# Expert weights fetched as couples of parts, in rows of 16 KB instead of 8 KB

## What is computed

```python
def expert_block(args):
    xb, e = args
    hb = jax.nn.silu(xb @ w_g[e]) * (xb @ w_u[e])
    return hb @ w_d[e]
...
y = y_pad[dest] * gates[order][:, None].astype(y_pad.dtype)
out = jnp.zeros((t, d), xt.dtype).at[token_idx[order]].add(y)
```

## Time and profile before

| | |
|---|---|
| median of 3 runs | 1832.19 us (1831.79 to 1833.74) |
| the profiled execution | 1832.44 us |
| its span, first to last instruction | 1830.6 us |
| around the span | 1.8 us |
| TensorE busy over the span | 98% |
| VectorE, ScalarE busy | 71%, 57% |
| DMA, mean over the span | 246 GB/s |
| granted clock of TensorE, mean | 0.994 |

### The profile page before, as it was taken

How to read it: one execution, slowest core, us unless ns; L and a number is a source line. 1 busy time by engine, 2 the same in 40 slices (tenths; PEclk the granted TensorE clock), 3 DMA queues, 4 the chain that set the end, 5 groups by cost and what they waited for, 6 DMA issues and landing times.

```text
span 1830.6 us, 22547 instructions
## 1 busy us (share of the span) xinstructions
PE 1789.4 (98%) x9273; PEld 1514.8 (83%) x9273; DVE 1292.6 (71%) x1295; ACT 1034.5 (57%) x1069; POOL 103.3 (6%) x106
## 2 busy tenths in 40 slices
PE   8998999999999999999999999999999999999998
PEld 7987788888788887888899888888888899888886
DVE  5876799999999998655468755546554778755554
ACT  5554698889888886544344444435443544444442
POOL 1010110111010100000000000000000100000000
PEclk9999999999999999999999999999999999999999
DMA  9842689999999999555464355545554754446550
GB/s 350 257 150 104 257 348 417 410 400 417 397 414 411 415 408 370 198 184 184 147 252 149 137 186 184 187 169 217 187 187 168 267 194 151 173 161 220 185 188 39
DMA packets 69885, 450.25 MB, mean 246 GB/s; under 512 B 11276, under 2 KB 11640, under 8 KB 18577
## 3 DMA queue, kind: packets, MB, share of 16 engines
q1 hardware_dynamic: 59744, 425.44, 61.5%
q0 software_dynamic: 9824, 22.78, 4.0%
q10 hardware_dynamic: 208, 0.54, 0.1%
HBM read 448.50 MB, written 14.16 MB: 253 GB/s over the span
## 4 chain that ended last, share of the span: by engine, by line
PE 78%; DMA 8%; DVE 7%; ACT 3%; issue 2%; POOL 0%; ACTq 0%; POOLq 0%; SPq 0%; DVEq 0%
PE PS L484 22%; PE PS L486 22%; PE PS L485 21%; DMA ring<-in_wt 8%; PE PS L1607 6%; DVE wl L462 4%; PE PS L1613 2%; PE PS L2223 1%; ACT wh L453 1%; DVE morel L462 1%; PE PS L523 1%; PE PS L2749 1%; ACT yr L1955 1%; PE PS L1598 1%; ACT moreh L453 1%
## 5 line engine op out<-in xcount | busy, mean ns | idle before, releaser
L462 DVE TENSOR_TENSOR wl<-ring,wh 128x2048 fp32r<-128x2048 f32 (+1 forms) x348 | 791.0, 2279 | 293.5 <-ACT wh L453 293.1
L453 ACT ACTIVATE wh<-ring 128x2048 fp32r<-128x2048 f32 (+1 forms) x348 | 661.6, 1907 | 307.2 <-PE PS L486 270.1
L484 PE MATMUL PS<-wh,XTh 128*128 128x512 f32 x952 | 379.2, 398 | 6.0 <-DVE XTl L567 3.0
L486 PE MATMUL PS<-wh,XTl 128*128 128x512 f32 x952 | 372.5, 391 | 0.0
L485 PE MATMUL PS<-wl,XTh 128*128 128x512 f32 x952 | 372.1, 391 | 0.0
L484 PEld LDWEIGHTS PS<-wh,XTh 128*128 128x128 f32 x952 | 179.4, 188 | 43.8 <-DVE wl L462 4.0
L486 PEld LDWEIGHTS PS<-wh,XTl 128*128 128x128 f32 x952 | 179.2, 188 | 38.1
L485 PEld LDWEIGHTS PS<-wl,XTh 128*128 128x128 f32 x952 | 179.6, 189 | 35.3 <-issue 0.2
L1607 PE MATMUL PS<-wh,xgT 128*128 128x512 f32 x384 | 155.4, 405 | 0.6 <-DVE xgT L1816 0.4
L1607 PE MATMUL PS<-wl,xgT 128*128 128x512 f32 x384 | 151.1, 394 | 0.0
L484 PE MATMUL PS<-XTh,wh 128*128 128x256 f32 (+2 forms) x480 | 138.0, 288 | 0.1
(11 more groups left out here) (445 smaller groups left out, 2546.4 us busy)
## 6 DMA issues: line engine op xcount, KB each, us to landing
ring<-in_wt SPq DMA_DIRECT2D x392, 1024.0 KB, 5.9
park<-in_wt SPq DMA_DIRECT2D x6, 1024.0 KB, 5.8
xtmp<-in_norm_g POOLq DMA_DIRECT2D x6, 512.0 KB, 5.7
ring<-in_wt SPq DMA_DIRECT2D x4, 512.0 KB, 7.6
toep<-frow POOLq DMA_DIRECT2D x1, 2048.0 KB, 55.6
y_d<-in_zero POOLq DMA_DIRECT2D x1, 2048.0 KB, 37.2
yy<-y_d POOLq DMA_DIRECT2D x4, 512.0 KB, 5.3
bv<-in_b_b_in POOLq DMA_DIRECT2D x1, 1536.0 KB, 7.6
```

Of the source, the lines that this page charges most:

```text
L453: s.activation(k.pieces(i)[0], k.raw(i), ACT.Copy).then_inc(*k.w_hi.up(i))
L462: v.tensor_tensor(l, k.raw(i), h.bitcast(F32), ALU.subtract).then_inc(*k.w_lo.up(i))
L484: pe.matmul(o, lhsT=left[0], rhs=right[0], start=first, stop=False)
L486: return pe.matmul(o, lhsT=left[1], rhs=right[0], start=False, stop=final)
```

## The change

Expert parts that aren't parked are fetched two at a time, as a couple: one DMA of 2 MiB brings two parts that follow each other. For this, `packed_weights` lays the rows of a couple side by side, so that each partition reads 16 KB in one row. There are three places for couples, `two0`, `two1` and `two2`: four of the five ring places make two of them, and the room of XT makes the third (with the old parks park2 and park3 gone from there; park2 moves to the fifth ring place). A couple is issued when the second part of the couple three before it has been split. Both its parts count as landed together. Outside the experts the ring works as before. The first five parts of f0 wait for other parts than before, and ScalarE waits, ahead of its first write to XT in f0, until the last expert part has been split.

```diff
 def packed_weights(inputs):
 
-    out = []
-    for nk, w, blocks in weight_parts()[0]:
...
+    parts, at = weight_parts()
+    firsts, out = set(couples(at)), []
...
+        out.append(x.reshape(nk, 128, w).transpose(1, 0, 2).reshape(128, -1))
+    rows = [np.concatenate(out[i:i + 2], 1) if i in firsts else x for i, x in enumerate(out) if i - 1 not in firsts]
+    return np.concatenate([x.reshape(-1) for x in rows])
+
+
+def couples(at):
+
+    m = at["moe"]
+    return [m + 5, m + 8, m + 10] + list(range(m + 14, at["f0"], 2))
...
+        self.two = [at(f"two{x}", o, 2 * PART) for x, o in enumerate((9768, 15912, 5672))]
...
+        if self.moe_part(i):
+            n, x = self.couple(i)
+            return self.two[n % 3][:, PART * x:PART * x + PART]
...
+    def left_place(self, i):
+
+        f0 = self.at["f0"]
+        if self.moe_part(i):
+            n, _ = self.couple(i)
+            return self.couples[n - 3] + 1 if n > 2 else (self.at["moe"] - 1, None, self.at["moe"] + 2)[n]
+        if f0 <= i < f0 + RING:
+            return (self.at["moe"] + 7, f0 - 6, f0 - 5, f0 - 4, f0 - 3)[i - f0]
+        return i - RING
...
+    elif k.moe_part(i):
+        n, x = k.couple(i)
+        if x == 0:
+            if n == 1:
+                sp.wait_ge(*k.moe.pe.at("lg"))
+            else:
+                sp.wait_ge(*k.w_lo.at(k.left_place(i)))
+            sp.dma_start(k.two[n % 3], k.couple_in(i)).then_inc(*k.d[f"two{n % 3}"].up(i))
+        return
     elif i >= RING:
-        sp.wait_ge(*k.w_lo.at(k.line[k.line.index(i) - RING]))
+        sp.wait_ge(*k.w_lo.at(k.left_place(i)))
...
     split_hi(s, k, k.after[a])
+    s.wait_ge(*k.w_lo.at(k.at["f0"] - 1))
     enter_high(s, k, m, 0, 0)
```

More of the change, by code:

```diff
@@ L181, in packed_weights @@
 def packed_weights(inputs):
-    out = []
-    for nk, w, blocks in weight_parts()[0]:
-        x = np.concatenate([inputs[name][at][r0:r0 + 128 * nk, c0:c1] for name, at, r0, c0, c1 in blocks], 1)
-        out.append(x.reshape(nk, 128, w).transpose(1, 0, 2).reshape(-1))
-    return np.concatenate(out)
+    parts, at = weight_parts()
+    firsts, out = set(couples(at)), []
+    for nk, w, blocks in parts:
+        x = np.concatenate([inputs[name][at_][r0:r0 + 128 * nk, c0:c1] for name, at_, r0, c0, c1 in blocks], 1)
+        out.append(x.reshape(nk, 128, w).transpose(1, 0, 2).reshape(128, -1))
[4 more added lines that the diff above has]
+    return [m + 5, m + 8, m + 10] + list(range(m + 14, at["f0"], 2))
 def split_plan(n, spans):
@@ L212 @@
 LANDINGS = ("ident", "cst", "rows", "x0", "x1", "rel", "ones", "mem", "b", "toep", "sel", "gmix", "gmem", "ga", "gl", "gc", "late", "gf", "gn", "wr", "xn", "zero", "yy", "bt", "ki",
-            "wsp", "bsp", "bcol", "bv", "gain", "out", "w0", "half0", "half1", "park0", "park1", "park2", "park3", "park4", "park5", "w1", "w2", "w3", "w4", "xg0", "xg1", "yd0", "yd1",
+            "wsp", "bsp", "bcol", "bv", "gain", "out", "w0", "half0", "half1", "park0", "park1", "park2", "park4", "park5", "two0", "two1", "two2", "w1", "w2", "w3", "w4", "xg0", "xg1", "yd0", "yd1",
             "rest_xg", "rest_w", "rest_yd")
@@ L237, in __init__ @@
         first = self.at["moe"]
-        self.parked = {first + SPLIT: "park0", first + SPLIT + 1: "park1", first + 7: "park2", first + 8: "park3",
-                       first + 12: "park4", first + 13: "park5"}
-        self.line = [i for i in range(len(self.parts)) if i not in self.parked]
+        self.parked = {first + SPLIT: "park0", first + SPLIT + 1: "park1", first + 7: "park2", first + 12: "park4",
+                       first + 13: "park5"}
+        self.couples = couples(self.at)
         self.part_at = [0] + list(itertools.accumulate(128 * nk * w for nk, w, _ in self.parts))
@@ L345, in __init__ @@
         self.parks = {"park0": here("park0", 14768, PART), "park1": here("park1", 12720, PART),
-                      "park2": at("park2", 15912, PART), "park3": at("park3", 17960, PART),
+                      "park2": at("park2", 13864, PART),
                       "park4": here("park4", 6824, PART), "park5": here("park5", 0, PART)}
+        self.two = [at(f"two{x}", o, 2 * PART) for x, o in enumerate((9768, 15912, 5672))]
         self.hs = here("hs", 0, 4, 256)
@@ L405, in raw, with moe_part, couple, ring_place @@
             return self.parks[self.parked[i]]
-        return self.ring[:, self.line.index(i) % RING, 0:self.parts[i][0] * self.parts[i][1]]
+        if self.moe_part(i):
+            n, x = self.couple(i)
+            return self.two[n % 3][:, PART * x:PART * x + PART]
+        return self.ring[:, self.ring_place(i), 0:self.parts[i][0] * self.parts[i][1]]
+    def moe_part(self, i):
+        return self.at["moe"] + SPLIT <= i < self.at["f0"]
+    def couple(self, i):
+        n = max(n for n, first in enumerate(self.couples) if first <= i)
+        return n, i - self.couples[n]
+    def ring_place(self, i):
+        return i % RING if i < self.at["f0"] else (i - self.at["f0"] + 4) % RING
+    def left_place(self, i):
[6 more added lines that the diff above has]
+        return i - RING
+    def landed(self, i):
+        if self.moe_part(i) and i not in self.parked:
+            n, x = self.couple(i)
+            return self.d[f"two{n % 3}"].at(i - x)
+        return self.landing(i).at(i)
     def landing(self, i):
-        return self.d[self.parked[i] if i in self.parked else f"w{self.line.index(i) % RING}"]
+        return self.d[self.parked[i] if i in self.parked else f"w{self.ring_place(i)}"]
+    def couple_in(self, i):
+        return self.a["wt"][self.part_at[i]:self.part_at[i + 2]].rearrange("(p n) -> p n", p=128)
     def part_in(self, i):
+        if self.moe_part(i) and i not in self.parked:
+            _, x = self.couple(i)
+            return self.couple_in(i - x)[:, PART * x:PART * x + PART]
         return self.a["wt"][self.part_at[i]:self.part_at[i + 1]].rearrange("(p n) -> p n", p=128)
@@ L435, in load_part @@
         sp.wait_ge(*k.cross.pe.at("pt1"))
-    elif k.parked.get(i) in ("park2", "park3"):
-        sp.wait_ge(*k.moe.pe.at("lg"))
+    elif k.parked.get(i) == "park2":
+        sp.wait_ge(*k.w_lo.at(k.at["moe"]))
     elif i in k.parked:
@@ L451, in split_hi @@
         s.wait_ge(*k.w_used.at(k.left[i]))
-    s.wait_ge(*k.landing(i).at(i))
+    s.wait_ge(*k.landed(i))
     s.activation(k.pieces(i)[0], k.raw(i), ACT.Copy).then_inc(*k.w_hi.up(i))
@@ L3059, in sync_program @@
     first_sync(sp, k)
-    ahead = k.at["moe"] + SPLIT + RING + 4
+    ahead = k.at["moe"] + 12
     for i in range(k.at["moe"], ahead):
```

## The result

| | before | after |
|---|---|---|
| median of the runs, us | 1832.07 (1831.79 to 1833.74, 4 runs) | 1883.73 (1882.75 to 1883.80, 4 runs) |
| span of the profiled execution, us | 1830.6 | 1880.9 |
| granted clock of TensorE, mean | 0.994 | 0.983 |

The change makes the kernel 2.8% slower: ratio 1.0279, 95% interval 1.0261 to 1.0297, +51.7 us. That lies outside the predicted range of 1824 to 1844 us.

What follows compares the result with a forecast made beforehand. The prediction took the saturated DMA engines, with TensorE close behind, to bound the experts. Longer rows -6.0, later landing +2.5 and late requests +5.6 summed to +2.1 us, for a median of 1834.3 us, range 1824 to 1844.

Steps and rivals of the forecast that it cites:

- What bounds the kernel before: Experts, 259.0 to 697.2 us: DMA engines always busy, TensorE close behind; faster loads could give at most 11.1 us.
- the place that the earlier trace had named: Split at 569.37 us waits for its part's landing; `us` and TensorE's `fold_up` wait behind it, about once a period.
- Longer rows (-6.0 us): Expert weight stream: a 16 KB row takes 0.610 us against 0.628 for two of 8 KB; -6.0 us taken.
- The end at 0: Upper end of the longer-row estimate, 0 to -12.1 us: the fixed share may be hidden already, so no gain.
- rival D: Weight stream: a 16 KB row is moved as two of 8 KB; +8.1 us, 1840.3 us, chance 0.04.
- Rival E: Weight stream: each DMA has its own cost, so half as many let TensorE set the pace; 1821.1 us, chance 0.05.
- The first part of a couple lands later (+2.5 us): Experts: the first part counts as landed 2.5 us later, shifting TensorE once, paid at the stage's end; +2.5 us.
- Requests come late (+5.6 us): Experts: late couple requests leave holes of 0 to 1.2 us a period; 0.4 taken, +5.6 us for 14 periods.
- The request that I gave no reserve: Request after VectorE's split behind the token copies: 2.5 us of reserve, made nil by the 2.5 us shift.
- Edits at nothing: Ahead of 259 us, XT's new wait, first f0 parts, gathers, and from f0 on: no cost.
- B: Experts: engines wait for SyncE at most couples; 0.85 us a period gives 1840.6 us, 1.2 gives 1845.5; chance 0.31.
- Its reserve row: Experts: 8.1 us from request to landing against a lone part's 4.9; the 3.2 us reserve becomes 0 to 1.1.

Runs made afterwards that it cites:

- the two timed kernels: The change timed again, 1882.1 us, and the change with each couple fetched as two DMAs in 8 KB rows that land together, 1877.6 us.
- seven places: Kernel before with five ring places and two in XT's room: couples in 16 KB rows, 1827.4 us; single parts in 8 KB rows, 1826.1 us.
- seven single places: Kernel before with five ring places and two in XT's room, each part requested and landing by itself: 1826.1 us, ratio 0.9961.
- the kernel with rows of 8 KB: The change with each couple fetched as two DMAs in 8 KB rows, still landing together: 1880.1 us at first, 1877.6 us timed again.

## Why the prediction was wrong, step by step

**What bounds the kernel before** held: TensorE's pace of 30.5 us a period ahead of 259 us is unchanged (30.4 measured), the loss lies wholly in the saturated stretch, and it shows at the place that the earlier trace rows had named.

**Longer rows (-6.0 us).** The duration was right. The records give 611 ns for a row of 16 KB against the 0.610 us computed, and the queue of the weights moved 9908 packets from 280 to 680 us instead of 22086, so rival D is out. The gain is not there: 414 GB/s either way once the queue is full, and 1827.4 us with long rows against 1826.1. By the means in the full queue a row of 16 KB took 629 ns and two of 8 KB 634. The end at 0 was the true one, and in the change as it stands the sign is the other, 4.6 us by the two timed kernels. Rival E, a cost of each DMA, isn't seen either: with seven places 88 DMAs instead of 155 (280 to 680 us) gave the same periods of 30.9 us.

**The first part of a couple lands later (+2.5 us): the first step that failed.** I wrote that this is "a shift of TensorE against the stream, not a slower pace, and it is paid once". But the place is freed by the very splits that are shifted, so a later split is a later request and a later landing. I had carried the shift into the reserve of one request and held the landings fixed. Taking away only the joint landing took 1877.6 back to 1832.8 us (the latter a single time): 45 us, 3.2 us in each of 14 periods.

**Requests come late (+5.6 us): the second, and the one that decided.** The need was put at 2.4 us ahead of the landing of what is queued before, from a lone part's 4.9 us. Full pace needs 4.5 to 5 us. With my figure a couple would land 7.3 us after its request: (7.3 + 7.8) / 3 = 5.0 us, just under the stream's 5.2 (31.30 / 6), hence small holes at the tightest place. With the measured 9.8 it is (9.8 + 7.6) / 3 = 5.8 us, and 12% over. The size of a hole was wrong in kind too: I walked each request against a fixed schedule and bounded the hole by the scatter of landings, 1.2 us a period. In a closed loop each hole moves the next request, and nothing catches up. Measured are 3.73 us a period, nine times the 0.4 taken.

The places were about as tight as I had them. The request that I gave no reserve waits for the first split after the copies of tokens. In the turn shown these are:

```profile
617.40 4.49 DVE L519 TENSOR_TENSOR wl<-two,wh 128x2048 fp32r<-128x2048 f32 x2 [0.16 <-ACT wh L510]
619.73 0.33 SPq L496 DMA_DIRECT2D two<-in_wt  x1
```

It came 3.7 us ahead of the landing at 623.39, and over the 11 periods from 280 to 680 us 2.6 us ahead in the mean. The request at 613.54, one of those to which I gave some reserve, came 2.0 us ahead of the landing at 615.55, and in the mean 2.6. I had taken 2.4 for a place with no reserve. So the lead was what I took it for; the need was about twice as large.

**Edits at nothing** held: outside the 14 periods nothing was lost (1.9 us less in these two executions, which their scatter can make), XT's new wait and the first parts of f0 included. Missing was the clock, 6 us, which falls after the new waits.

**The rivals.** The sign that I gave for B (the queue runs dry: DMA share under 0.97, periods over 31.6 us) is what is seen, 0.95 and 35.0 us. B was the true mechanism at 0.31, priced at 0.85 to 1.2 us a period instead of 3.7. Its reserve row was there: 8.1 us from request to landing with five places. Set in the loop, five places x 2.61 us = 13.0 us, of which 4.9 remained for the splits; six parts in couples give 15.7 us (6 x 2.61), and 7.8 for the splits leaves 7.9 for a DMA of twice the bytes. That leaves 0.6 us above my own 7.3, for a delay that no row of a couple had shown. The 7.8 is read off the changed kernel, but the rows before give nearly the same: 4.9, and 2.5 for the joint landing, make 7.4, and the margin is then 1.0 us. That sum could have been made blind, and so thin a margin should have made B the likeliest.

## What to carry to other kernels

When the places for prefetched blocks are few, write the loop down: request to landing, plus landing to the instruction that frees the place, over the number of places, and compare it with the stream's own pace; if it is near, anything that lengthens one term (a joint landing, a release by the second half of a block) comes back in every round. Take request to landing from blocks in the full stream and not from lone ones (9.8 us here, where the lone part's 4.9 gave 7.3). More places, or an earlier release, is the remedy; seven single places (1826.1 us) are the fastest of all kernels run here, and six (1826.9 us) can't be told from them.

## What the runs showed of the hardware

- The 16 DMA engines end one DMA of the weight stream unevenly: 2.1 us between the first and the last in the change, 2.3 without any indirect DMA beside it, against 0.44 us for a lone one. With more queued it grows, to 7.1 us with seven single places.
- With three places of 2 MiB, couples asked for less than 2.4 us ahead of the landing before came 6.6 us after it, and those asked for more than 4.5 us ahead 5.2 us after it.
- A row of 16 KB took 611 ns in the changed kernel and one of 8 KB 309 ns in the kernel with rows of 8 KB (medians, 280 to 680 us); in the kernel before one of 8 KB took 313. In a full queue both move 414 GB/s.
- After TensorE's longer waits for `us` (2.26 us in the row shown) its clock fell to 1.2 GHz for some microseconds; with matmuls of no use in their place the mean was 1.00, which was worth 6.0 us.
